# Latent heads of a two-block layer: where the exponent table is loaded, when a gate bank is read, and in which bank finished pairs are turned

## The chip, the cores and the metric

The kernel runs on one core of one Trainium2 chip. The metric is the device time of one execution in microseconds (us). Five engines work side by side: TensorE (PE in the profile, with its weight loads as PEld), VectorE (DVE), ScalarE (ACT), GpSimd (POOL) and SyncE (SP), which issues the transfers of the weights. Each engine takes its instructions strictly in the order in which the program lists them, and an instruction waits there until its semaphores have reached their values.

## What is computed

Two transformer blocks in a row on 512 tokens of width 1024, all in float32 precision. The first block has a gated convolution, a sparse attention, a cross attention and a feed-forward. The second block is the one that the change touches: its mixer has an mLSTM (4 heads) beside a latent attention (8 heads), whose outputs are joined and projected.

```python
def causal_block_attention(q, k, v):
    ...
    sc = jnp.einsum('bhqd,bkhd->bhqk', qblk.astype(jnp.float32), kf) * scale
    sc = jnp.where(kpos[None, :] <= qpos[:, None], sc, -jnp.inf)
    p = jax.nn.softmax(sc, axis=-1)
    return jnp.einsum('bhqk,bkhd->bqhd', p, vf)

def token_mixer(a, ...):
    proj = a @ w_in                       # q, k, v, output gate o_ml and gates of the mLSTM, latents
    ...
    h_ml = mlstm_chunkwise(...)
    h_ml = rmsnorm(h_ml, ...) * jax.nn.sigmoid(o_ml)
    ...
    h_mla = causal_block_attention(q, k, kv[..., MLA_NOPE:])
    return jnp.concatenate([h_ml, h_mla], axis=-1) @ w_out
```

## The kernel before

**Weights.** All matrices are streamed as 256 chunks of 512 KB through a ring of four slots (`w_raw`). SP issues chunk c when the products of chunk c-4 are done (`chunk_done`). ACT rounds a chunk to `w_hi` (`round_to`, L1205, with the cast at L1203), POOL subtracts to get the rest `w_lo` (L405), and PE multiplies in three products (hi by hi, hi by lo, lo by hi, L494). One chunk against all 512 tokens is 8 steps of three products of 512 columns.

**The latent tiles.** The attention of 8 heads runs over 32 tiles: tile n is head n // 4 and query block n % 4, so it has n % 4 + 1 blocks of 128 keys. For a tile, PE makes the scores (`latent_scores`, banks 4 and 5), DVE adds the mask and finds the maximum (`latent_mask`), ACT takes the exponential (`latent_exps`), PE turns it (`latent_turn`, bank 6), ACT copies it (`latent_turned`), PE multiplies it with the values (`latent_values`, bank 2) and DVE scales the result into `o_rows` (`latent_scaled`). In loop n PE makes the scores of tile n+2, turns tile n and makes the values of tile n-1.

**What runs beside them.** Bank 7 (`BESIDE_BANK`) gets 56 steps of three products: four row blocks of the mLSTM's values (steps 0 to 31) and three chunks of its output gate (steps 32 to 55, `gate_step`). The table `BESIDE` says how many of these steps PE does in loop n, and `BESIDE_DONE` in which loop DVE reads the finished bank (`beside_out`; the gates by `gate_out`, L2278). The first gate chunk, OA, is made ahead of the tiles, in another bank, and its reading by DVE stands between the first masks and loop 0. The four mLSTM heads follow each other every seven loops (`ml_step`); of their steps PE makes products with `sT`, ACT makes `decay`, squares and a root (which needs another function table than the exponential), and DVE the rest.

**Pairs.** After 8 tiles two heads are finished. PE turns the pair's rows (`pair_turn`, L1017) into bank 2, ACT casts them to `mix_hi` (`pair_hi`, L1639), and DVE subtracts to get `mix_lo` (`pair_lo`, L2411). Bank 2 is also the bank of the values, so in the loops n = 9, 17 and 25 the values of tile n-1 are put off to the next loop, where they wait until `pair_lo` has read the bank (`o_ready`). The fourth pair comes behind the last tile. Behind the tiles the output projection (`wo_step`) begins, and the last mLSTM head is turned between its steps (`ml_turn`, L967).

## Time and profile before

| | us |
|---|---|
| median of 3 runs | 1586.34 |
| lowest and highest of them | 1584.93, 1586.52 |
| time of the profiled execution | 1584.47 |
| its span, from first to last instruction | 1582.7 |
| mean granted TensorE clock | 0.997 of full speed |

The profile is one execution. The stage that the change touches lies between about 1035 and 1180 us from the start of the span. Starts and durations are of the profile; the end of a matmul is modelled and lies some 0.16 us behind the point at which the next one can start, so the idle time that a row names in brackets is smaller than the time lost between starts.

### The profile page before, as it was taken

Reading aid. Unit: us, or ns where it says so; the run is one execution under the profiler, and the core shown is the slowest. Engines: PE = TensorE matmul, PEld = TensorE weight load, DVE = VectorE, ACT = ScalarE, POOL = GpSimd, SP = SyncE. Lnnn points to the kernel's source line nnn. Section 1 sums busy time; section 2 is a strip of 40 time slices with the busy share of each in tenths; the row PEclk is TensorE's granted clock in tenths of the full one; section 3 lists DMA queues with packets and bytes.
Section 4 is the critical chain, followed back from the end, with each engine's and each line's share of the span. In section 5 each row is a group of like instructions: output and inputs, shape, how many; then the busy total and the mean of one; then the engine's idle time right before and its main releaser. Section 6 shows DMA issues by size and latency. Waiting matters only on the chain.

```text
span 1582.7 us, 21175 instructions
## 1 busy us (share of the span) xinstructions
PE 1546.7 (98%) x7370; PEld 1280.5 (81%) x7370; DVE 838.8 (53%) x1483; ACT 652.6 (41%) x1065; POOL 662.9 (42%) x301
## 2 busy tenths in 40 slices
PE   7999999999999999999999999999999999999997
PEld 6888888778788877888888888777779888888887
DVE  5689999887784445442111134767645612121125
ACT  5553333444462445433233245455754523232331
POOL 4454444323334432444444445442524544444442
PEclk9999999999999999999999999999999999999999
DMA  5243323221333322333333333221112333333332
...
DMA packets 41125, 144.57 MB, mean 91 GB/s; under 512 B 4565, under 2 KB 6741, under 8 KB 40793
## 3 DMA queue, kind: packets, MB, share of 16 engines
...
q14 instruction: 29, 0.23, 0.1%
...
## 4 chain that ended last, share of the span: by engine, by line
PE 90%; issue 3%; DVE 3%; ACT 2%; POOL 1%; DMA 1%; SPq 0%; DVEq 0%; POOLq 0%; ACTq 0%
PE bank L494 88%; DMA w_raw<-in_stream 1%; PE bank L604 1%; POOL w_lo L405 1%; POOL res L470 1%; DVE x_sq L1807 1%; PE bank L999 0%; DVE bias L1880 0%; DVE xu_lo L1816 0%; ACT w_hi L1203 0%; ACT kT L1368 0%; DVE ffy L2574 0%; ACT probs L1236 0%; DVE kh L2377 0%; DVE q_ml L2351 0%
## 5 line engine op out<-in xcount | busy, mean ns | idle before, releaser
L405 POOL TENSOR_TENSOR w_lo<-w_raw,w_hi 128x1024 fp32r<-128x1024 f32 x254 | 614.4, 2419 | 847.3 <-ACT w_hi L1203 847.1
L1203 ACT CAST w_hi<-w_raw 128x1024 fp32r<-128x1024 f32 x256 | 268.6, 1050 | 501.6 <-DMA w_raw<-in_stream 501.5
L494 PE MATMUL bank<-a_hi,w_hi 128*128 128x512 f32 (+1 forms) x1120 | 445.0, 397 | 2.9 <-DVE a_lo L2487 1.7
L494 PE MATMUL bank<-a_hi,w_lo 128*128 128x512 f32 (+1 forms) x1120 | 431.6, 385 | 0.0
L494 PE MATMUL bank<-a_lo,w_hi 128*128 128x512 f32 (+1 forms) x1120 | 431.2, 385 | 0.0
L494 PEld LDWEIGHTS bank<-a_hi,w_hi 128*128 128x128 f32 x1120 | 210.5, 188 | 50.7 <-issue 4.1
L494 PEld LDWEIGHTS bank<-a_lo,w_hi 128*128 128x128 f32 x1120 | 210.5, 188 | 45.7 <-issue 3.6
L494 PEld LDWEIGHTS bank<-a_hi,w_lo 128*128 128x128 f32 x1120 | 210.3, 188 | 42.2
L494 PE MATMUL bank<-b_hi,w_hi 128*128 128x512 f32 (+1 forms) x640 | 244.3, 382 | 0.0
L494 PE MATMUL bank<-b_hi,w_lo 128*128 128x512 f32 (+1 forms) x640 | 242.3, 379 | 0.0
L494 PE MATMUL bank<-b_lo,w_hi 128*128 128x512 f32 (+1 forms) x640 | 242.2, 378 | 0.0
L494 PEld LDWEIGHTS bank<-b_hi,w_hi 128*128 128x128 f32 x640 | 120.4, 188 | 22.7 <-issue 0.2
L494 PEld LDWEIGHTS bank<-b_lo,w_hi 128*128 128x128 f32 x640 | 120.4, 188 | 22.6 <-issue 0.2
L494 PEld LDWEIGHTS bank<-b_hi,w_lo 128*128 128x128 f32 x640 | 120.4, 188 | 22.6
L2113 DVE SCALAR_TENSOR_TENSOR ff_t<-bank,rstd 128x512 f32<-128x512 f32 x64 | 44.2, 690 | 149.1 <-PE bank L494 149.1
L2116 DVE TENSOR_TENSOR b_lo<-ff_f,b_hi 128x512 fp32r<-128x512 f32 x64 | 47.2, 738 | 86.8 <-ACT b_hi L1472 86.8
L1944 DVE SCALAR_TENSOR_TENSOR bank<-conv_in,cols,bank 128x512 f32<-128x512 f32 x114 | 82.3, 750 | 1.6
L2124 DVE TENSOR_TENSOR res<-bank,res 128x512 f32<-128x512 f32 x32 | 22.1, 691 | 108.7 <-PE bank L494 108.7
L1923 DVE SCALAR_TENSOR_TENSOR bank<-conv_in,cols,bank 128x512 f32<-128x512 f32 x116 | 76.6, 749 | 0.0
L1470 ACT ACTIVATE ff_f<-ff_t 128x512 f32<-128x512 f32 x64 | 40.5, 632 | 85.6 <-DVE ff_t L2113 85.6
L2124 DVE TENSOR_TENSOR ffy<-bank,ffy 128x512 f32<-128x512 f32 x20 | 13.8, 692 | 84.4 <-PE bank L494 84.4
L1245 ACT COPY probsT<-bank 128x256 f32<-128x256 f32 (+3 forms) x48 | 19.7, 409 | 58.0 <-PE bank L604 58.0
...
## 6 DMA issues: line engine op xcount, KB each, us to landing
w_raw<-in_stream SPq DMA_DIRECT2D x256, 512.0 KB, 3.5
...
```

Source lines behind the costliest of these rows:

```text
L405: nc.gpsimd.tensor_tensor(w_lo[:, j, :], w_raw[:, j, :], w_hi[:, j, :].bitcast(F32), ALU.subtract).then_inc(w_lo_done, 1)
L470: nc.gpsimd.tensor_tensor(res[:, j, t], res[:, j, t], mixed[:, j, t], ALU.add).then_inc(sems["post_added"], 1)
L494: return nc.tensor.matmul(o, l, r, start=start, stop=stop)
L604: m = nc.tensor.transpose(turned_bank(U)[:, r], probs[:, U % 2, r], ident)
L1203: A.copy(w_hi[:, slot, :], w_raw[:, slot, :]).then_inc(w_hi_done, 1)
L1245: A.copy(probsT[:, U % 2, r], turned_bank(U)[:, r]).then_inc(sems["pT_copied"], 1)
L1470: A.activation(ff_f[:, j % 2, :], ff_t[:, j % 2, :], ACT.Square).then_inc(sems["f_sq"], 1)
L1923: V.scalar_tensor_tensor(out=blk(conv_io, e, 0, T) if last else acc, in0=u, scalar=w, in1=acc, op0=ALU.mult, op1=ALU.add).then_inc(sems["c ...
L1944: m = V.scalar_tensor_tensor(out=out, in0=u, scalar=w, in1=acc if start is None else start, op0=ALU.mult, op1=ALU.add)
L2113: V.scalar_tensor_tensor(out=ff_t[:, j % 2, :], in0=bank, scalar=0.0, in1=rstd[:, :], op0=ALU.max, op1=ALU.mult).then_inc(evac_dve, 1)
L2116: V.tensor_tensor(b_lo[:, j, :], ff_f[:, j % 2, :], b_hi[:, j, :].bitcast(F32), ALU.subtract).then_inc(sems["f_ready"], 1)
L2124: V.tensor_tensor(dst[:, i, :], bank, dst[:, i, :], ALU.add).then_inc(evac_dve, 1)
```

## The change

It has three parts. First, ACT gets a dummy exponential of one column (`table_first`) ahead of `round_to(CH["OA"])`, so that the table is loaded there. Second, DVE reads the OA bank (`gate_out(0, ...)`) ahead of the last of three gate-row operations, not behind it, and the small memset of `v_ml` goes ahead of both. Third, the first three pairs are turned into bank 7 in loops 10, 17 and 25 (`PAIR_TURN_AT`), in which `BESIDE` has no step; the values are no longer put off, and instead the first step of each of the last three gate chunks waits for `pair_lo` (`o_ready`). `pair_hi` now stands behind the copy and the exponential of its loop on ACT, and `pair_lo` behind `latent_scaled` on DVE. `BESIDE`, `BESIDE_DONE` and `cast_at` are laid anew: from loop 11 on steps move to later loops, five of them into loops 28 to 30.

```diff
```diff
--- before.py
+++ after.py
@@ -144,8 +144,9 @@
 ML_END = ML_EVERY * (ML_HEADS - 1) + ML_START + 13
 
 
-BESIDE = [3, 3, 2, 4, 4, 4, 4, 3, 3, 2, 0, 2, 2, 2, 1, 1, 2, 1, 2, 1, 1, 1, 2, 1, 2, 1, 1, 1]
-BESIDE_DONE = {2: 0, 4: 1, 6: 2, 9: 3, 15: 4, 21: 5, 27: 6}
+BESIDE = [3, 3, 2, 4, 4, 4, 4, 3, 3, 2, 0, 1, 2, 2, 1, 1, 1, 0, 1, 1, 2, 1, 1, 1, 1, 0, 1, 2, 2, 2, 1]
+PAIR_TURN_AT = {10: 0, 17: 1, 25: 2}
+BESIDE_DONE = {2: 0, 4: 1, 6: 2, 9: 3, 16: 4, 24: 5, 30: 6}
 BESIDE_BANK = 7
 CONV_AT = {0: 0, 4: 1}
 SILU_AT = {4: (0, 2), 14: (1, 3)}
@@ -351,6 +352,9 @@
                 return ps[2][:, :], c_hi[:, G, :], c_lo[:, G, :]
             return ps[2][:, :], xo_hi[:, G - X_G, :], xo_lo[:, G - X_G, :]
 
+        def pair_bank(p):
+            return ps[BESIDE_BANK if p < MLA_HEADS // 2 - 1 else 2]
+
         def turned_bank(U):
             return ps[6 + U % 2]
 
@@ -923,6 +927,7 @@
                 c, o = CH["OM"] + j, O["OM"] + j
                 if k == 0:
                     pe.wait_ge(evac_dve, o - DVE_FROM)
+                    pe.wait_ge(sems["o_ready"], MLA_G + j + 1)
                 chunk(c, c % RING, None, BESIDE_BANK, a_hi, a_lo, ks=range(k, k + 1))
 
             def beside(n):
@@ -1002,10 +1007,7 @@
             def latent_values(n):
                 h, nk = n // 4, n % 4 + 1
                 pe.wait_ge(sems["pT_copied"], U0 + n + 1)
-                if n % 8 == 0:
-                    pe.wait_ge(sems["o_ready"], MLA_G + n // 8)
-                else:
-                    pe.wait_ge(sems["o_scaled"], n)
+                pe.wait_ge(sems["o_scaled"], n)
                 for kb in range(nk):
                     m = mm(ps[2][:, 0:MLA_V], probsT[:, n % 2, kb * P:(kb + 1) * P],
                            v_mla[kb // 2][:, kb % 2, h * MLA_V:(h + 1) * MLA_V], kb == 0, kb == nk - 1)
@@ -1013,8 +1015,10 @@
 
             def pair_turn(p):
                 pe.wait_ge(sems["o_scaled"], 8 * p + 8)
+                if p < MLA_HEADS // 2 - 1:
+                    pe.wait_ge(evac_dve, O["OM"] + p - DVE_FROM)
                 for qb in range(TB):
-                    m = nc.tensor.transpose(ps[2][:, qb * P:(qb + 1) * P], o_rows[p][:, qb, :], ident)
+                    m = nc.tensor.transpose(pair_bank(p)[:, qb * P:(qb + 1) * P], o_rows[p][:, qb, :], ident)
                 m.then_inc(sems["o_turned"], 1)
 
             c, o = CH["OA"], O["OA"]
@@ -1028,14 +1032,11 @@
             for n in range(4 * MLA_HEADS):
                 if n + 2 < 4 * MLA_HEADS:
                     latent_scores(n + 2)
-                turning = n >= 8 and n % 8 == 1
-                if n >= 8 and n % 8 == 2:
-                    latent_values(n - 2)
+                if n in PAIR_TURN_AT:
+                    pair_turn(PAIR_TURN_AT[n])
                 ml_hook(n)
-                if turning:
-                    pair_turn(n // 8 - 1)
                 latent_turn(n)
-                if n >= 1 and not turning:
+                if n >= 1:
                     latent_values(n - 1)
                 ml_turns(n)
             latent_values(4 * MLA_HEADS - 1)
@@ -1555,6 +1556,7 @@
                 for i in range(4):
                     A.copy(qh[rr, 4 * t + i, :], qrot[ROPE * i:ROPE * (i + 1), t, :]).then_inc(sems["q_roped"], 1)
             round_to(CH["UKV"])
+            A.activation(table_first[:, :], eps, ACT.Exp)
             round_to(CH["OA"])
 
             def ml_step(h, st):
@@ -1590,7 +1592,7 @@
                     act.wait_ge(sems["ml_gated"], h + 1)
                     A.copy(mix_hi[h], hml[:, h % 2, :]).then_inc(sems["ml_hi"], 1)
 
-            cast_at = {8: CH["VM"] + 1, 9: CH["VM"] + 2, 10: CH["VM"] + 3, 11: CH["OM"], 16: CH["OM"] + 1, 22: CH["OM"] + 2, 28: CH["WO"]}
+            cast_at = {8: CH["VM"] + 1, 9: CH["VM"] + 2, 10: CH["VM"] + 3, 11: CH["OM"], 18: CH["OM"] + 1, 26: CH["OM"] + 2, 32: CH["WO"]}
 
             def ml_hook(n):
                 if n == 0:
@@ -1636,18 +1638,18 @@
 
             def pair_hi(p):
                 act.wait_ge(sems["o_turned"], p + 1)
-                A.copy(mix_hi[ML_HEADS + p], ps[2][:, :]).then_inc(sems["o_hi"], 1)
+                A.copy(mix_hi[ML_HEADS + p], pair_bank(p)[:, :]).then_inc(sems["o_hi"], 1)
 
             latent_exps(0)
             latent_exps(1)
             open_gate(0)
             round_to(CH["VM"])
             for n in range(4 * MLA_HEADS):
-                if n >= 8 and n % 8 == 1:
-                    pair_hi(n // 8 - 1)
                 latent_turned(n)
                 if n + 2 < 4 * MLA_HEADS:
                     latent_exps(n + 2)
+                if n in PAIR_TURN_AT:
+                    pair_hi(PAIR_TURN_AT[n])
                 ml_hook(n)
             pair_hi(MLA_HEADS // 2 - 1)
             for n in range(4 * MLA_HEADS, ML_END):
@@ -2408,29 +2410,26 @@
 
             def pair_lo(p):
                 dve.wait_ge(sems["o_hi"], MLA_G + p + 1)
-                V.tensor_tensor(mix_lo[ML_HEADS + p], ps[2][:, :], mix_hi[ML_HEADS + p].bitcast(F32), ALU.subtract
+                V.tensor_tensor(mix_lo[ML_HEADS + p], pair_bank(p)[:, :], mix_hi[ML_HEADS + p].bitcast(F32), ALU.subtract
                                 ).then_inc(sems["o_ready"], 1)
 
             latent_mask(0)
             latent_mask(1)
             chained(V.tensor_tensor(gt[g4, 0, :], gt[g4, 0, :], gt[g4, 3, :], ALU.subtract))
             chained(V.tensor_tensor_scan(gt[g4, 4, :], gt[g4, 5, :], gt[g4, 0, :], 0.0, ALU.add, ALU.max))
-            V.tensor_tensor(gt[g4, 3, :], gt[g4, 3, :], gt[g4, 4, :], ALU.add).then_inc(sems["gates_done"], 1)
+            V.memset(v_ml[:, :, :, ML_V:ML_V + 1], 1.0).then_inc(sems["ml_ones"], 1)
             dve.wait_ge(chunk_done, CH["OA"] + 1)
             gate_out(0, ps_of(O["OA"]))
-            V.memset(v_ml[:, :, :, ML_V:ML_V + 1], 1.0).then_inc(sems["ml_ones"], 1)
+            V.tensor_tensor(gt[g4, 3, :], gt[g4, 3, :], gt[g4, 4, :], ALU.add).then_inc(sems["gates_done"], 1)
             for n in range(4 * MLA_HEADS):
                 latent_inverse(n)
                 if n + 2 < 4 * MLA_HEADS:
                     latent_mask(n + 2)
-                turning = n >= 8 and n % 8 == 1
-                if n >= 8 and n % 8 == 2:
-                    latent_scaled(n - 2)
-                if turning:
-                    pair_lo(n // 8 - 1)
                 ml_first(n)
-                if n >= 1 and not turning:
+                if n >= 1:
                     latent_scaled(n - 1)
+                if n in PAIR_TURN_AT:
+                    pair_lo(PAIR_TURN_AT[n])
                 ml_rest(n)
             latent_scaled(4 * MLA_HEADS - 1)
             pair_lo(MLA_HEADS // 2 - 1)
```
```

The order of the instructions shows the three places of which the prediction speaks. Ahead of tile 0, on ACT, before (`w_hi` is the cast of a weight chunk, the first `probs` rows are the exponentials of tiles 0 and 1, `ogate` the gate of OA):

```order
L1203 CAST w_hi<-w_raw 128x1024 [waits chunk_done,raw_landed3]
L1628 ACT_TABLE_LOAD [waits p_inv,pT_ready]
L1628 ACTIVATE probs,rowsum<-bank,negmax 128x128 [waits s_masked]
L1628 ACTIVATE probs,rowsum<-bank,negmax 128x256 [waits p_inv,pT_ready,s_masked]
L1537 ACTIVATE ogate<-ogate 128x512 [waits evac_dve]
L1539 ACTIVATE ogate<-ogate,half_gain 128x512 [waits o_gated]
L1203 CAST w_hi<-w_raw 128x1024 [waits chunk_done,raw_landed0]
```

The same place after the change; the load stands ahead of the cast whose data the transfer brings last:

```order
L1559 ACT_TABLE_LOAD
L1559 ACTIVATE table_first<-consts 128x1
L1204 CAST w_hi<-w_raw 128x1024 [waits chunk_done,raw_landed3]
L1630 ACTIVATE probs,rowsum<-bank,negmax 128x128 [waits p_inv,pT_ready,s_masked]
L1630 ACTIVATE probs,rowsum<-bank,negmax 128x256 [waits p_inv,pT_ready,s_masked]
L1538 ACTIVATE ogate<-ogate 128x512 [waits evac_dve]
L1540 ACTIVATE ogate<-ogate,half_gain 128x512 [waits o_gated]
L1204 CAST w_hi<-w_raw 128x1024 [waits chunk_done,raw_landed0]
```

What moved is the table load, from directly ahead of the first exponential to ahead of the cast. On DVE, at the same time, before (`gt` are rows of the gates, the row with `ogate<-bank` reads the OA bank):

```order
L2416 TENSOR_TENSOR gt<-gt 4x512
L2417 SCALAR_TENSOR_TENSOR gt<-gt 4x512 [waits row_step]
L2418 TENSOR_TENSOR gt<-gt 4x512 [waits row_step]
L2278 TENSOR_TENSOR ogate<-bank,ssq 128x512 [waits chunk_done]
L2421 MEMSET v_ml 128x16
L2400 RECIPROCAL rowinv<-rowsum 128x1 [waits p_ready]
L2394 ISA bank,negmax<-bank,consts 128x384 [waits p_ready,s_ready]
```

And after; the third row with `gt` now stands behind the reading of the bank:

```order
L2418 TENSOR_TENSOR gt<-gt 4x512
L2419 SCALAR_TENSOR_TENSOR gt<-gt 4x512 [waits row_step]
L2420 MEMSET v_ml 128x16 [waits row_step]
L2280 TENSOR_TENSOR ogate<-bank,ssq 128x512 [waits chunk_done]
L2423 TENSOR_TENSOR gt<-gt 4x512
L2402 RECIPROCAL rowinv<-rowsum 128x1 [waits p_ready]
L2396 ISA bank,negmax<-bank,consts 128x384 [waits p_ready,s_ready]
```

What moved is that one row, behind the bank's reading. On PE, loops 9 to 11, before (`o_rows` is the turning of pair 0, `v_mla` with `probsT` the values, the last row the first gate step in bank 7; the first of the four transposes of the turning is the row ahead of these):

```order
L1017 MATMUL bank<-consts,o_rows_162 128x128 x3
L999 MATMUL bank<-consts,probs 128x128 [waits pT_copied,p_ready]
L999 MATMUL bank<-consts,probs 128x128
L494 MATMUL bank<-kh,qh 128x128 [waits q_roped,rope_done,p_ready]
L494 MATMUL bank<-v_mla_127,probsT 128x64 [waits o_ready,pT_copied]
L494 MATMUL bank<-v_ml,sT 128x129 [waits ml_ones,evac_dve,ml_sT]
L999 MATMUL bank<-consts,probs 128x128 [waits pT_copied,p_ready]
L999 MATMUL bank<-consts,probs 128x128 x2
L494 MATMUL bank<-v_mla_127,probsT 128x64 [waits o_scaled,pT_copied]
L494 MATMUL bank<-v_mla_127,probsT 128x64
L494 MATMUL bank<-kh,qh 128x256 [waits p_ready]
L494 MATMUL bank<-a_hi,w_hi 128x512 [waits w_lo_done,evac_dve]
```

And after, up to the same gate step:

```order
L1004 MATMUL bank<-consts,probs 128x128
L498 MATMUL bank<-v_mla_127,probsT 128x64 [waits o_scaled,pT_copied]
L498 MATMUL bank<-kh,qh 128x128 [waits q_roped,rope_done,p_ready]
L1021 MATMUL bank<-consts,o_rows_162 128x128 [waits evac_dve,o_scaled]
L1021 MATMUL bank<-consts,o_rows_162 128x128 x3
L498 MATMUL bank<-v_ml,sT 128x129 [waits ml_ones,evac_dve,ml_sT]
L1004 MATMUL bank<-consts,probs 128x128 [waits pT_copied,p_ready]
L1004 MATMUL bank<-consts,probs 128x128 x2
L498 MATMUL bank<-v_mla_127,probsT 128x64 [waits o_scaled,pT_copied]
L498 MATMUL bank<-v_mla_127,probsT 128x64
L498 MATMUL bank<-kh,qh 128x256 [waits p_ready]
L498 MATMUL bank<-a_hi,w_hi 128x512 [waits w_lo_done,o_ready,evac_dve]
```

What moved: the turning stands behind tile 9 and the scores of tile 12, the values of tile 8 no longer wait for `o_ready`, and the gate step does. On ACT, loops 16 and 17, before (`mix_hi` is the cast of pair 1):

```order
L1203 CAST w_hi<-w_raw 128x1024 [waits chunk_done,raw_landed1]
L1567 DMA mrow<-m_rows 128x512 [waits ml_decay,ml_diag]
L1537 ACTIVATE ogate<-ogate 128x512 [waits evac_dve]
L1539 ACTIVATE ogate<-ogate,half_gain 128x512 [waits o_gated]
L1639 CAST mix_hi_150<-bank 128x512 [waits o_turned]
L1635 COPY probsT<-bank 128x256 [waits pv_done,pT_ready]
L1628 ACTIVATE probs,rowsum<-bank,negmax 128x512 [waits p_inv,pT_ready,s_masked]
L1583 ACTIVATE ml_square,mcol<-bank 128x128 [waits ml_out]
L1583 ACTIVATE ml_square,mcol<-bank 128x128 x3
L1635 COPY probsT<-bank 128x384 [waits pv_done,pT_ready]
```

And after:

```order
L1569 DMA mrow<-m_rows 128x512 [waits ml_decay,ml_diag]
L1637 COPY probsT<-bank 128x256 [waits pv_done,pT_ready]
L1630 ACTIVATE probs,rowsum<-bank,negmax 128x512 [waits p_inv,pT_ready,s_masked]
L1641 CAST mix_hi_150<-bank 128x512 [waits o_turned]
L1585 ACTIVATE ml_square,mcol<-bank 128x128 [waits ml_out]
L1585 ACTIVATE ml_square,mcol<-bank 128x128 x3
L1538 ACTIVATE ogate<-ogate 128x512 [waits evac_dve]
L1540 ACTIVATE ogate<-ogate,half_gain 128x512 [waits o_gated]
L1637 COPY probsT<-bank 128x384 [waits pv_done,pT_ready]
L1630 ACTIVATE probs,rowsum<-bank,negmax 128x128 [waits p_inv,pT_ready,s_masked]
L1204 CAST w_hi<-w_raw 128x1024 [waits chunk_done,raw_landed1]
```

What moved: the cast of pair 1 stands behind the copy and the exponential of its loop, the gate's two operations behind the mLSTM's squares, and the weight cast to loop 18.

## Rows read from the trace of the kernel before

**Rows 1.** The page's first part: busy us, share of the span, instructions

```profile
PE 1546.7 (98%) x7370; PEld 1280.5 (81%) x7370; DVE 838.8 (53%) x1483; ACT 652.6 (41%) x1065; POOL 662.9 (42%) x301
```

**Rows 2.** PE's waits, 1040 to 1190: us in total, times, longest

```profile
PE bank L494 <- DVE mix_lo L2411: 3.2, 3, 1.1
```

**Rows 3.** Timeline, loops 9 to 12, PE, POOL and DVE

```profile
1094.86 0.39 PE L494 MATMUL bank<-kh,qh 128*128 128x128 f32 x2
1096.30 0.41 PE L494 MATMUL bank<-v_mla,probsT 128*128 128x64 f32 x2 [1.05 <-DVE mix_lo L2411]
...
1097.39 4.89 POOL L405 TENSOR_TENSOR w_lo<-w_raw,w_hi 128x1024 fp32r<-128x1024 f32 x2 [2.56 <-ACT w_hi L1203]
...
1098.70 3.86 DVE L2377 COPY kh<-krT 32x512 f32<-32x512 f32 x2
...
1104.23 1.08 PE L494 MATMUL bank<-v_mla,probsT 128*128 128x64 f32 x8 [0.82 <-DVE o_rows L2406]
```

**Rows 4.** Stretch by engine: us, PE, PEld, DVE, ACT, POOL, clock, DMA, GB/s

```profile
1053.30:1056.70 3.40, 3.19 (x8) 2.54 (x9) 2.16 (x9) 2.38 (x3) 0.81 (x1) 0.50 0.11 45
1094.30:1096.40 2.10, 1.05 (x10) 0.89 (x9) 0.94 (x2) 1.56 (x5) 0.54 (x1) 1.00 0.64 168
```

**Rows 5.** PE's timeline before tile 0: start, us, instruction, [idle before it]

```profile
1050.11 0.39 PE L494 MATMUL bank<-a_hi,w_lo 128*128 128x512 f32 x1
1051.20 0.91 PE L494 MATMUL bank<-kh,qh 128*128 128x384 f32 x2 [0.69 <-ACT probs L1628]
1053.51 0.76 PE L494 MATMUL bank<-w_hi,a_hi 128*128 128x512 f32 x1 [1.40 <-DVE ogate L2278]
...
1056.91 0.40 PE L494 MATMUL bank<-w_hi,a_lo 128*128 128x512 f32 x1
```

**Rows 6.** The same stretch, timeline of ACT, POOL and DVE

```profile
1048.32 1.05 ACT L1203 CAST w_hi<-w_raw 128x1024 fp32r<-128x1024 f32 x1 [2.89 <-DMA w_raw<-in_stream]
...
1049.39 1.28 ACT L1628 ACT_TABLE_LOAD   x1
...
1049.45 2.78 POOL L405 TENSOR_TENSOR w_lo<-w_raw,w_hi 128x1024 fp32r<-128x1024 f32 x1 [1.56 <-ACT w_hi L1203]
...
1050.10 2.67 DVE L2418 TENSOR_TENSOR gt<-gt 4x512 f32<-4x512 f32 x1
...
1052.69 0.67 DVE L2278 TENSOR_TENSOR ogate<-bank,ssq 128x512 f32<-128x512 f32 x1
```

**Rows 7.** The memsets of `q_ml` (min/median/max ns), and POOL at 1107

```profile
L2385 DVE MEMSET q_ml<- x4: 485/485/485, 1070.2 to 1108.4; 64x512 f32 x4
...
1107.09 2.04 POOL L434 TENSOR_TENSOR res<-res,cols 128x512 f32<-128x512 f32 x2
```

**Rows 8.** Timeline, loops 16 to 18: PE, DVE, ACT

```profile
1116.04 0.86 PE L494 MATMUL bank<-kh,qh 128*128 128x384 f32 x2
...
1117.42 2.66 DVE L2351 SCALAR_TENSOR_TENSOR q_ml<-q_ml,qk_ml 64x512 f32<-64x512 f32 x2
1120.11 1.66 DVE L2351 SCALAR_TENSOR_TENSOR qk_ml<-k_tanh,qk_ml 128x512 f32<-128x512 f32 x1
...
1123.47 0.38 ACT L1635 COPY probsT<-bank 128x256 f32<-128x256 f32 x1
1123.61 0.69 DVE L2411 TENSOR_TENSOR mix_lo<-bank,mix_hi 128x512 fp32r<-128x512 f32 x1 [0.72 <-ACT mix_hi L1639]
1123.74 0.70 ACT L1628 ACTIVATE probs<-bank,negmax 128x512 f32<-128x512 f32 x1
...
1124.45 0.41 PE L494 MATMUL bank<-v_mla,probsT 128*128 128x64 f32 x2 [1.05 <-DVE mix_lo L2411]
1124.66 0.47 PE L494 MATMUL bank<-a_hi,w_hi 128*128 128x512 f32 x1
```

**Rows 9.** Timeline behind the last tile: PE, ACT, DVE, PE

```profile
1167.63 0.66 PE L1017 MATMUL bank<-consts,o_rows 128*128 128x128 f32 x4 [0.45 <-DVE o_rows L2406]
...
1170.07 0.17 DVE L2319 SCALAR_TENSOR_TENSOR mcol<-mcol 128x4 f32<-128x4 f32 x1
```

## The prediction

> **What bounds the kernel now.** I read the page's busy times first: PE is busy for 98% of the span [rows 1], so nothing that another engine does counts unless PE waits for it. Then the waits of PE alone, in the stretch that the change touches: PE waited 3.2 us for `mix_lo`, three times, once at each of the first three pairs [rows 2]. The brackets understate what is lost. For pair 0 the row says 1.05 [rows 3], but the scores ahead started at 1094.86 and take 0.22, and the next product started at 1096.30: 1.22 us between starts. Summed in that way, from one start to the next against the usual 0.23 us of a product, I find 13.4 us lost between 1050 and 1168: 4.1 around the first tiles, 6.6 in loops 10 to 26, 2.7 in the last loops. This is all that the change can win. Last the clock: for 3.4 us from 1053.30 on PE was granted half of it, 1.2 of 2.4 GHz; around pair 0 it kept the whole [rows 4].
>
> **Part 1, the table load and the OA bank.** Ahead of the first step in bank 7 stand two waits [rows 5]. The scores of tile 2 wait for the first exponential, which waits for the table load of 1.28 us; and the first step waits for DVE to read OA's bank, which DVE does only at 1052.69, since the gate row ahead of it took 2.67 us beside a subtraction of POOL's [rows 6]. After the change the load falls into ACT's 2.89 us of idle time ahead of the cast at 1048.32, which waits for its transfer and so does not move. The first exponential then starts near 1049.4 and not at 1050.69, and the scores of tile 2 find it done. The Trainium skill (ScalarE: Activation LUTs, "ACT is a hardware spline evaluator", under what a load costs) states 1283 ns for the load and about 1380 ns of drain behind it. The trace has the 1.28 but starts the exponential 0.02 us behind it. By the page's 2.66 us the gain would not be larger than the sum below, because the bank is what comes last; and the load with its drain would still fit into the 2.89.
>
> DVE can read the bank when OA's last product ends, 1050.11 + 0.39 = 1050.50 [rows 5]; the reading is a form with one operand in the accumulator banks, which took 0.67 us at 1052.69. The memset now ahead of it isn't held up by POOL: those of `q_ml` took 485 ns at 1070 with POOL idle and 485 ns at 1108 with POOL busy [rows 7]. From the start of the reading to PE's first step it was 1053.51 - 1052.69 = 0.82 us, so PE starts at 1051.3: 2.2 us earlier. And PE then idles for 0.4 us and not 2.4 in those 3 us, so the clock shouldn't fall: nine products took 3.64 us (eight starts from 1053.51 to 1056.91, and one more), at 0.23 each and 0.1 for the first it is 2.15: 1.5 us. What is late next: the last value chunk's rest is needed in loop 2; its transfer starts with OA's end and takes some 3.5 us, an estimate, cast and subtraction 1.05 + 2.78 more [rows 6], which is 1057.8, when PE gets there. I count 0.1. The gate row that was passed (now ending near 1052.8 again, held by the same subtraction of POOL's) is needed in loop 1 only. **Sum -3.6** (bounds -2.1, if the clock falls all the same, and -4.1, all that was lost).
>
> **Part 2, pairs 0 and 1.** No instruction is added or removed: four turnings, a cast and a subtraction per pair, as before. The wait isn't removed either. It moves from the values to the first gate step one loop later, and the chain in it grows: the turning's cast stands on ACT behind the copy and the exponential of its loop. For pair 0 my walk along the queues gives 2.1 us of waiting where there were 1.22. But a little later both versions wait for the same thing: DVE's two copies of `kh` took 3.86 us beside two subtractions of POOL's, and PE got the next values only at 1104.23 [rows 3]. The weight cast that feeds POOL comes some 0.6 us earlier, so that point comes 0.8 us earlier, but with one step (three products, 0.69 us) less done. Net -0.1.
>
> For pair 1 I count from the scores of tile 18 at 1116.04. Before, PE was at the gate step of loop 18 at 1124.66, 8.6 us later [rows 8]. After: DVE has mask 18, then the three operations of L2351, which took 4.35 us from 1117.42 beside POOL and start at the same point, since both engines wait for the same scores: done at +5.7. Then the gate bank's reading, which the new table puts here (0.69), `sT` and the scaling of tile 15: +6.7. Only then may PE turn the pair; by its own work it is there at +3.9, so it idles for 2.9 us. Turning 0.44, two products with `sT` 0.22, turning of tile 17 0.22: +7.7. ACT: 0.2 to start, copy 0.27 (1123.47 to 1123.74), exponential 0.67 (0.70 less an overlap) [rows 8], cast 0.6: +9.45. DVE and back to PE 0.84, as from the `mix_lo` at 1123.61 to the row at 1124.45: +10.3. That is 1.7 us later, with two steps (1.4 us) less done: +3.1. **Sum of both pairs +3.0** (bounds 0, if other work covers the longer chain, and +4).
>
> **Part 3, pair 2 and the end.** Pair 2 goes like pair 0, without the wait for the copies; two table loads that stood directly ahead of the copy of tile 25 now come beside gate steps. **+0.2.** The last loops: before, PE had no step in loops 28 to 31 and waited five times, the last with 0.45 in brackets [rows 9]; 2.7 us between starts. Five steps now lie in loops 28 to 30 and cover the first three waits: **-1.3** (bounds -2.7 and 0). Behind the last pair ACT gets a weight cast of 1.05 us ahead of the last head's root. The turning of that head stands between steps of the projection and has a little slack, so I take half of the 1.05: **+0.5** (bounds 0 and +2.3, below).
>
> **Part 4, the clock.** PE would idle for 2.9 us ahead of pair 1 and, after 1.2 us of work, for 2.1 more. Around OA, idling for 2.4 of 3 us brought it to half [rows 4, 5]; at pair 0, 1.2 of the 1.44 us up to 1096.30 didn't [rows 3, 4]. I take one fall, at the price that the nine products paid plus a little for the small ones: **+1.7** (bounds 0 and +2.6).
>
> **Sum.** -3.6 + 3.0 + 0.2 - 1.3 + 0.5 + 1.7 = +0.5 us. The profiled execution of 1584.47 us would become 1585.0. The median of before is 1586.34, so 1.9 us above the profiled execution; the same step on it gives **1586.8 us**. A measurement of this kernel can tell about 0.2%, 3.2 us, from no change, so my forecast is no change that can be told.
>
> **Rivals.**
> - *The pair waits are covered.* Part 1 stands, the pairs cost no more than before and the clock stays up: -3.6 + 0 + 0.2 - 1.3 + 0.5 = -4.2, 1582.1 us. For it: part 1 is the surest term, and ACT is busy for 41% of the span [rows 1], so away from the pairs little is queued ahead of a cast. Against it: in loops 16 and 17 the chain over DVE is longer than PE's work by 2.9 us even with nothing added.
> - *The clock falls at all three pairs* (the slower side). The waits of 2.1 and 2.3 us at pairs 0 and 2 lie between the 1.2 that left the clock up and the 2.4 that brought it down. Each further fall costs 1.7: +0.5 + 3.4 = +3.9, 1590.2 us. [...]
> - *A shared port at the end.* The cast moved behind the last pair gives POOL a subtraction that starts near 1169.95; DVE's small product of two operands from the same memory started at 1170.07 [rows 9]. The gate row of only four partitions was held from 1050.10 until POOL was through [rows 6]. If this one is held too, the root comes 1.8 us later still: +2.3, 1588.6 us. The Trainium skill (SBUF — State Buffer, "SBUF: two separate sides") gives this as a rule: VectorE with two SBUF inputs and GpSimd share one pair of ports, and whoever starts first holds it for the whole instruction. By that rule, the trace agrees in [rows 6], and only the 0.1 us between the two starts decides.
> - *The change doesn't do what it says:* the load is hidden, but the clock falls around OA as before. Then part 1 is -2.1: +2.0, 1588.3 us.
>
> **How the numbers follow.** Forecast 0.45 (1584 to 1589.5 of its own); covered 0.25; three falls 0.15; port 0.10; clock around OA 0.05. The range from 1581.5 to 1591 takes in all but the outer halves of the first two rivals. Faster by over 0.2%: 0.25, the covered case. Slower by over 0.2%: 0.15 of the clock, and 0.07 for the port and the forecast's upper end with a second mishap: 0.22. Within: 0.53.
>
> **What would show it.** Part 1: the load near 1045.5, PE's first step in bank 7 near 1051.3, no half clock near 1053. Part 2: PE waits at the first gate steps for `mix_lo`, longer than 1.05 in brackets each; ahead of pair 1's turning PE waits for DVE. Part 3: no waits in loops 28 to 30. Part 4: a half-clock stretch near 1118 to 1123. If PE doesn't wait ahead of pair 1, or the waits at the gate steps are under 1 us, part 2 is wrong and the time falls towards 1582.

## The result

| | us |
|---|---|
| before, median of 9 runs | 1586.12 (1584.39 to 1586.84) |
| after, median of 9 runs | 1590.05 (1588.37 to 1593.53) |
| ratio | 1.0027, 95% interval 1.0018 to 1.0035 |
| profiled execution after, and its span | 1590.11, 1588.3 |

The changed kernel is slower by 0.27%, 3.9 us of the medians. The time lies inside the range given, but it isn't the forecast (1586.8, no change that can be told): it is slower by more than a measurement's uncertainty. It lies 0.5 us above the forecast's own upper end (1589.5); that the range of 9.5 us takes it in says little for the sum. It falls almost on the rival of three clock falls (1590.2), and yet not for that rival's reasons.

The page of the changed kernel has PE 3.4 us busier than [rows 1], with the same 7370 matmuls:

```profile
PE 1550.1 (98%) x7370; PEld 1282.8 (81%) x7370; DVE 842.3 (53%) x1483; ACT 652.7 (41%) x1066; POOL 661.4 (42%) x301
```

PE's waits in the changed kernel from 1040 to 1190 (total, times, longest) answer to [rows 2]. The three waits for `mix_lo` are now named "issue"; they stand at the gate steps, 0.05 to 0.1 us behind `mix_lo`. Two are new, ahead of a turning of a pair (L1021) and of the last head (L972):

```profile
PE bank L498 <- issue: 5.6, 3, 1.9
PE bank L1021 <- DVE o_rows L2408: 3.1, 2, 2.7
PE bank L498 <- DVE o_rows L2408: 1.2, 2, 0.7
PE bank L972 <- DVE ml_rows L2342: 0.6, 1, 0.6
```

**The first place.** Timeline before tile 0, which answers to [rows 5, 6]:

```profile
1047.38 1.28 ACT L1559 ACT_TABLE_LOAD   x1
1048.68 0.20 ACT L1559 ACTIVATE table_first<-consts 128x1 f32<-128x1 f32 x1
...
1052.03 0.39 PE L498 MATMUL bank<-a_hi,w_lo 128*128 128x512 f32 x1
...
1052.30 0.91 PE L498 MATMUL bank<-kh,qh 128*128 128x384 f32 x2
1052.46 0.69 DVE L2280 TENSOR_TENSOR ogate<-bank,ssq 128x512 f32<-128x512 f32 x1 [0.32 <-PE bank L498]
...
1053.07 1.70 DVE L2423 TENSOR_TENSOR gt<-gt 4x512 f32<-4x512 f32 x1
...
1053.30 0.47 PE L498 MATMUL bank<-w_hi,a_hi 128*128 128x512 f32 x1
```

From OA's last product to the first step in bank 7 it is 1.27 us, where it was 3.40. The dummy exponential starts 0.02 us behind the load's end. The Trainium skill (ScalarE: Activation LUTs, "ACT is a hardware spline evaluator") adds a drain of about 1.38 us to a load; it doesn't show here either.

**Pair 1.** Loops 16 to 18 of the changed kernel, PE, DVE and ACT, which answer to [rows 8]:

```profile
1114.99 2.66 DVE L2353 SCALAR_TENSOR_TENSOR q_ml<-q_ml,qk_ml 64x512 f32<-64x512 f32 x2
...
1117.69 1.64 DVE L2353 SCALAR_TENSOR_TENSOR qk_ml<-k_tanh,qk_ml 128x512 f32<-128x512 f32 x1
1119.25 0.68 DVE L2280 TENSOR_TENSOR ogate<-bank,ssq 128x512 f32<-128x512 f32 x1
...
1120.37 0.66 PE L1021 MATMUL bank<-consts,o_rows 128*128 128x128 f32 x4 [2.66 <-DVE o_rows L2408]
...
1121.48 0.44 PE L498 MATMUL bank<-kh,qh 128*128 128x128 f32 x2
...
1123.07 0.69 DVE L2413 TENSOR_TENSOR mix_lo<-bank,mix_hi 128x512 fp32r<-128x512 f32 x1 [1.03 <-ACT mix_hi L1641]
...
1123.86 0.76 PE L498 MATMUL bank<-a_hi,w_hi 128*128 128x512 f32 x1 [1.94 <-issue]
```

PE loses 2.8 us ahead of the turning and 2.1 ahead of the gate step (between starts), and the clock falls at 1122.55, within the second of these waits.

**The last head.** Behind the last tile, ACT, POOL, DVE and PE, which answers to [rows 9]:

```profile
1171.90 1.05 ACT L1204 CAST w_hi<-w_raw 128x1024 fp32r<-128x1024 f32 x1
...
1173.03 2.37 POOL L409 TENSOR_TENSOR w_lo<-w_raw,w_hi 128x1024 fp32r<-128x1024 f32 x1 [10.34 <-ACT w_hi L1204]
1173.16 2.27 DVE L2321 SCALAR_TENSOR_TENSOR mcol<-mcol 128x4 f32<-128x4 f32 x1
...
1177.29 0.66 PE L972 MATMUL bank<-consts,ml_rows 128*128 128x128 f32 x4 [0.62 <-DVE ml_rows L2342]
```

DVE's product on four columns starts 0.13 us behind POOL's subtraction and takes 2.27 us instead of 0.17.

**The clock.** Stretches of the changed kernel (the granted clock is the third column from the end), which answer to [rows 4]: none at the first place, one behind pair 1, one behind the last tile:

```profile
1050.50:1054.00 3.50, 3.42 (x14) 2.19 (x13) 3.06 (x5) 2.75 (x7) 2.16 (x1) 1.00 0.14 9
1122.50:1129.20 6.70, 5.34 (x17) 4.40 (x18) 3.34 (x18) 5.94 (x17) 1.20 (x1) 0.50 0.00 0
1170.40:1173.90 3.50, 3.50 (x11) 2.93 (x12) 1.79 (x6) 2.69 (x4) 0.87 (x1) 0.52 0.00 0
```

### The profile page after: what moved, and what is told of

Same layout as the page of the kernel before. It is cut to its first block, busy times and chain, and to the rows that moved or that the text cites. A ratio compares the mean times of both kernels' runs of the same rounds, so it can differ in the third digit from the quotient of the medians.

```text
span 1588.3 us, 21179 instructions
## 1 busy us (share of the span) xinstructions
PE 1550.1 (98%) x7370; PEld 1282.8 (81%) x7370; DVE 842.3 (53%) x1483; ACT 652.7 (41%) x1066; POOL 661.4 (42%) x301
## 3 DMA queue, kind: packets, MB, share of 16 engines
HBM read 141.43 MB, written 2.11 MB: 90 GB/s over the span
## 4 chain that ended last, share of the span: by engine, by line
PE 89%; DVE 4%; issue 3%; ACT 2%; POOL 1%; DMA 1%; SPq 0%; DVEq 0%; POOLq 0%; ACTq 0%
PE bank L498 87%; PE bank L608 1%; DMA w_raw<-in_stream 1%; POOL w_lo L409 1%; POOL res L474 1%; DVE x_sq L1809 1%; PE bank L1004 1%; DVE cq_rstd L1745 0%; DVE xu_lo L1818 0%; DVE bias L1882 0%; ACT w_hi L1204 0%; ACT kT L1369 0%; DVE cn_lo L2230 0%; DVE gt L2253 0%; DVE ffy L2573 0%
```

## The experiments

All ratios are to the kernel before on the same chip; their intervals reach 1.3 to 2.2 us to either side, so the runs can't tell two kernels apart that differ by about a microsecond. Shifts are read from one trace each: the start of the same matmul against the profile of before, in three pieces: from OA's last product to loop 9 (1050.11 to 1092.38 in the kernel before), from there to the turning of pair 3 (1167.63), and from there to 1180.01.

| kernel | to loop 9 | to pair 3 | end | stage | ratio (95%) |
|---|---|---|---|---|---|
| changed | -3.6 | +4.4 | +2.4 | +3.2 | 1.0027 (1.0018 to 1.0035) |
| e8 changed again | -3.6 | +5.1 | +2.5 | +3.9 | 1.0033 (1.0021 to 1.0046) |
| e1 part 1 | -3.6 | 0.0 | 0.0 | -3.6 | 0.9992 (0.9983 to 1.0001) |
| e2 changed without part 1 | -1.5 | +5.4 | +2.2 | +6.2 | 1.0049 (1.0035 to 1.0063) |
| e3 last cast at 33 | -3.6 | +4.4 | 0.0 | +0.8 | 1.0019 (1.0010 to 1.0028) |
| e4 pair's cast first | -3.6 | +3.1 | +2.0 | +1.5 | 1.0019 (1.0010 to 1.0028) |
| e5 new tables, old pairs | -3.7 | +3.0 | 0.0 | -0.7 | 1.0029 (1.0018 to 1.0041) |
| e6 products in loop 15 | -3.6 | +1.5 | +2.0 | -0.1 | 1.0010 (1.0001 to 1.0019) |
| e7 scan late, on before | -1.5 | +0.1 | 0.0 | -1.4 | 0.9991 (0.9982 to 1.0000) |
| e9 load only | -1.5 | 0.0 | 0.0 | -1.5 | 0.9996 (0.9987 to 1.0006) |
| e10 bank first only | -3.3 | 0.0 | +1.6 | -1.7 | 0.9996 (0.9987 to 1.0005) |
| e11 change mended | -3.7 | -1.8 | 0.0 | -5.5 | 0.9971 (0.9960 to 0.9982) |
| e12 part 1, scan, products | -3.4 | +0.8 | +1.6 | -1.1 | 0.9988 (0.9978 to 0.9997) |

**e1_part1 and e2_pairs_only** split the change in two. e1's edit on the kernel before (e2 takes the same lines out of the changed kernel):

```diff
             round_to(CH["UKV"])
+            A.activation(table_first[:, :], eps, ACT.Exp)
             round_to(CH["OA"])
...
-            V.tensor_tensor(gt[g4, 3, :], gt[g4, 3, :], gt[g4, 4, :], ALU.add).then_inc(sems["gates_done"], 1)
+            V.memset(v_ml[:, :, :, ML_V:ML_V + 1], 1.0).then_inc(sems["ml_ones"], 1)
             dve.wait_ge(chunk_done, CH["OA"] + 1)
             gate_out(0, ps_of(O["OA"]))
-            V.memset(v_ml[:, :, :, ML_V:ML_V + 1], 1.0).then_inc(sems["ml_ones"], 1)
+            V.tensor_tensor(gt[g4, 3, :], gt[g4, 3, :], gt[g4, 4, :], ALU.add).then_inc(sems["gates_done"], 1)
```

> Part 1 alone on the kernel before (table load ahead of the cast of OA, bank of OA read ahead of the third gate row, pairs and tables as before). My theory: this part did what was forecast, and all of the loss comes from the pairs. PE's first step in bank 7 comes 3.6 us earlier against the last product of OA, no half clock near 1053, no half clock near 1122 or 1170 either, and the time is 3.7 us below before: about 1582.4, ratio 0.9977. Rival: the half-clock stretches near 1122 and 1170 of the changed kernel belong to a stage that is run more densely from 1053 on, whatever the pairs do. Then they appear here too, and the time is 1584.5 to 1586, ratio 0.999 to 1.000.

> The changed kernel without part 1 (load directly ahead of the first exponential, OA bank read behind the third gate row), pairs and tables as in the changed kernel. My theory: the losses add up, so it is 3.7 us above the changed kernel: 1593.7, ratio to before 1.0048; half clock near 1053, at pair 1 and perhaps at the end. Rival: the clock falls at pair 1 only because it was not already low near 1053. Then the time is 1591 or less, ratio 1.003.

e1's trace shows the 3.6 us and no half clock in the stage, so both falls of the changed kernel come with the rest. But its runs give 1.3 us and not 3.7, and their interval takes in no change at all. e2 shows one reason: it has before's two waits at the first place, 0.73 and 1.69 us between starts, and its clock did not fall there (-1.5 in the table); e7, with the same order, had no fall there either. So in one of three traces with these waits the clock fell, the one of before, and 1.5 of my 3.6 us were that fall. A second reason lies in e1's own executions: the profiled one is the fastest of eleven (1582.50, mean clock 0.998), and the mean clock of all eleven is 0.9966, below the 0.9968 of before's on that chip. So the other ten, at 0.995 to 0.997, lost some clock that the trace doesn't show; where, no trace says. e10 and e12 below, its nearest relatives, lost 1.6 us of it near 1168. How much of the gap each reason makes stays open. e2's ratio came as expected, by another sum.

**e3_cast33** moves one cast:

```diff
-            cast_at = {8: CH["VM"] + 1, 9: CH["VM"] + 2, 10: CH["VM"] + 3, 11: CH["OM"], 18: CH["OM"] + 1, 26: CH["OM"] + 2, 32: CH["WO"]}
+            cast_at = {8: CH["VM"] + 1, 9: CH["VM"] + 2, 10: CH["VM"] + 3, 11: CH["OM"], 18: CH["OM"] + 1, 26: CH["OM"] + 2, 33: CH["WO"]}
```

> The changed kernel with the last weight cast of the stage one loop later (33 for 32), so behind the root of the last mLSTM head on ACT, and POOL's subtraction with it. My theory (shared port and the cast in front of the root cost 0.8 us at the last head): DVE's product on 4 columns takes 0.17 us again and not 2.27, PE no longer waits for the turning of the last head, the time is 0.8 us below the changed kernel: 1589.2, ratio to before 1.0020. The half clock near 1170 starts before the cast and stays. Rival: the cast's place costs nothing, since the slow clock alone makes PE late or early there; the time is that of the changed kernel, 1590.0, ratio 1.0025, and PE's wait ahead of the turning stays over 0.5 us.

Timeline of e3 at the place of the changed kernel's last rows:

```profile
1173.88 0.16 DVE L2321 SCALAR_TENSOR_TENSOR mcol<-mcol 128x4 f32<-128x4 f32 x1
...
1174.39 1.03 ACT L1204 CAST w_hi<-w_raw 128x1024 fp32r<-128x1024 f32 x1
...
1175.50 2.40 POOL L409 TENSOR_TENSOR w_lo<-w_raw,w_hi 128x1024 fp32r<-128x1024 f32 x1 [11.61 <-ACT w_hi L1204]
...
1176.09 0.60 PE L972 MATMUL bank<-consts,ml_rows 128*128 128x128 f32 x4
```

The product takes 0.16 us and PE waits for nothing. The gain in the trace is 2.4 us, larger than the 0.8 expected. The runs give 1.3 to 2.2 us (the changed kernel has 1.0027, and 1.0033 as e8 on another chip), with intervals that overlap e3's. e4 and e6 say why: there the clock stayed up behind the last tile, PE came to the turning sooner, and waited 2.0 us, as in these rows of e4:

```profile
1172.48 2.40 POOL L409 TENSOR_TENSOR w_lo<-w_raw,w_hi 128x1024 fp32r<-128x1024 f32 x1 [9.90 <-ACT w_hi L1204]
...
1172.61 2.30 DVE L2321 SCALAR_TENSOR_TENSOR mcol<-mcol 128x4 f32<-128x4 f32 x1
...
1176.77 0.66 PE L972 MATMUL bank<-consts,ml_rows 128*128 128x128 f32 x4 [1.81 <-DVE ml_rows L2342]
```

So the cast's place costs 2.0 us with a full clock; where the clock falls, slow products cover a part of it and the sum is 2.4.

**e4_hi_first** puts the pair's cast ahead on ACT:

```diff
+                if n in PAIR_TURN_AT:
+                    pair_hi(PAIR_TURN_AT[n])
                 latent_turned(n)
                 if n + 2 < 4 * MLA_HEADS:
                     latent_exps(n + 2)
-                if n in PAIR_TURN_AT:
-                    pair_hi(PAIR_TURN_AT[n])
```

> The changed kernel with the cast of the turned pair ahead of the copy and the exponential of its loop on ACT (as in the kernel before), everything else as changed. My theory (the wait at the first gate step is the chain turning, copy, exponential, cast, subtraction, and the operations queued ahead of the cast are its price): the wait ahead of the gate step falls from 2.1 us between starts to some 1.2 at each of the three pairs, the wait of 2.8 us ahead of pair 1's turning stays since it is DVE's; if the clock then still falls at pair 1, the time is 2.7 us below the changed kernel, 1587.3, ratio 1.0008; if it stays up, 2.5 less, 1584.8, ratio 0.9993. Rival: the copy that is now late makes the products with the values late, and the wait only moves: 1589.5 or more, ratio 1.002.

From the start ahead of a gate step to its own it was 2.13, 2.22 and 2.22 us at the three pairs in the changed kernel; here it is 1.40, 1.09 and 1.61. The wait ahead of pair 1's turning stayed at 2.8. But behind pair 0 the wait for `o_rows` grew from 0.84 to 1.58, which is the rival in part. The gain to pair 3 is 1.3 us.

**e5_tables_old_pairs** is e1 with the changed kernel's tables, the last cast at 33, and pairs as before (`cast_at` as in e3):

```diff
-BESIDE = [3, 3, 2, 4, 4, 4, 4, 3, 3, 2, 0, 2, 2, 2, 1, 1, 2, 1, 2, 1, 1, 1, 2, 1, 2, 1, 1, 1]
-BESIDE_DONE = {2: 0, 4: 1, 6: 2, 9: 3, 15: 4, 21: 5, 27: 6}
+BESIDE = [3, 3, 2, 4, 4, 4, 4, 3, 3, 2, 0, 1, 2, 2, 1, 1, 1, 0, 1, 1, 2, 1, 1, 1, 1, 0, 1, 2, 2, 2, 1]
+BESIDE_DONE = {2: 0, 4: 1, 6: 2, 9: 3, 16: 4, 24: 5, 30: 6}
```

> The kernel before with part 1 and the new tables of steps (five steps in loops 28 to 30), the last weight cast at loop 33, but the pairs turned in the bank of the values as before. My theory: the tables are worth 1.3 us at the end and the turning in bank 7 is all that costs (5.6 us and the clock at the end). So the time is 1.3 us below part 1 alone, ratio to before 0.9984; no half clock near 1122 or 1170; PE waits 1.2 us at each pair as before. Rival: the tables themselves (fewer steps in loops 11 to 25) are what lets PE idle and the clock fall; then it is 1.0005 or more, and a half-clock stretch lies between 1110 and 1130.

My theory fell here. Without any turning in bank 7, PE stands still in the same place (PE and DVE of e5):

```profile
1116.71 1.08 PE L494 MATMUL bank<-kh,qh 128*128 128x512 f32 x2
1117.77 1.64 DVE L2352 SCALAR_TENSOR_TENSOR qk_ml<-k_tanh,qk_ml 128x512 f32<-128x512 f32 x1
1119.33 0.68 DVE L2279 TENSOR_TENSOR ogate<-bank,ssq 128x512 f32<-128x512 f32 x1
...
1120.26 0.49 PE L494 MATMUL bank<-v_ml,sT 128*128 128x129 f32 x2 [2.48 <-DVE sT L2306]
...
1122.68 0.66 PE L494 MATMUL bank<-v_mla,probsT 128*128 128x64 f32 x2 [1.05 <-DVE mix_lo L2412]
```

and the clock falls behind it, in 1122.60:1126.00, as the granted 0.50 shows:

```profile
1122.60:1126.00 3.40, 3.32 (x13) 2.95 (x13) 1.32 (x10) 3.13 (x14) 0.00 (x0) 0.50 0.00 0
```

Two things in the tables do this, and no run parts them: loops 16 and 17 have two steps less to cover DVE's chain, and the reading of the gate bank (the 0.68 us in the rows) moves from loop 15 into that chain. e3 differs from e5 only in where the pairs are turned: its ratio of 1.0019 against 1.0029, with overlapping intervals, shows no cost of the turning in bank 7, while the traces of the stage have +0.8 against -0.7. The profiled execution of e5 is the fastest of its seven (1584.95; the median is 1590.0, and their mean clocks go from 0.997 down to 0.991, the slowest at 1592.27). Where the others lose the clock no trace shows.

**e6_twice15** takes the three products of DVE out of loop 16:

```diff
-TWICE_AT = {5: 0, 16: 1}
+TWICE_AT = {5: 0, 15: 1}
```

> The changed kernel with the three products of DVE that finish the silu of the second pair of query blocks (L2353, 4.3 us beside POOL) one loop earlier, in loop 15 and not 16; everything else as changed. My theory: these three operations ahead of the gate bank's reading, the sT and the scaling are the wait of 2.8 us ahead of pair 1's turning, and this wait with the 2.1 us behind it brings the clock down. So the wait ahead of the turning is under 0.8 us, part of it comes back as a wait of up to 1 us one loop earlier, no half clock lies near 1124, and the time is 3.5 to 4.5 us below the changed kernel, ratio to before 0.9999 to 1.0005. Rival A: the wait only moves one loop ahead with its full size, the clock falls there: ratio 1.0025. Rival B: the wait goes but the clock falls all the same, from the 2.1 us at the gate step alone: ratio 1.0015.

In loop 15 they take 2.5 us and not 4.3: POOL is idle from 1112.75 to 1114.25, where in the changed kernel two of its operations (2.48 us from 1114.62 on, then 1.71) run beside them:

```profile
1112.20 1.81 DVE L2353 SCALAR_TENSOR_TENSOR q_ml<-q_ml,qk_ml 64x512 f32<-64x512 f32 x2 [1.11 <-ACT q_ml L1618]
...
1114.04 0.69 DVE L2353 SCALAR_TENSOR_TENSOR qk_ml<-k_tanh,qk_ml 128x512 f32<-128x512 f32 x1
...
1115.12 0.49 PE L498 MATMUL bank<-q_ml,qk_ml 128*128 128x128 f32 x2 [0.31 <-DVE sT L2307]
...
1117.81 0.66 PE L1021 MATMUL bank<-consts,o_rows 128*128 128x128 f32 x4
...
1121.30 0.47 PE L498 MATMUL bank<-a_hi,w_hi 128*128 128x512 f32 x1 [1.95 <-issue]
```

The wait of 2.8 us is gone for one of 0.5. The ratio of 1.0010 lies midway between my theory's upper end (1.0005) and rival B (1.0015); the trace decides for B: the clock still falls, at 1121.79, with the wait of 2.1 us ahead of it alone.

**e7_scan_late.** Every trace with the order of before near 1030, ahead of the stage, loses 1.0 to 1.3 us there, the changed kernel's and e1's, e9's and e10's too; only that of before loses nothing. Its timeline, DVE and POOL:

```profile
1027.07 1.21 DVE L2251 TENSOR_TENSOR_SCAN gt<-gt 4x512 f32<-4x512 f32 x1
1027.12 3.37 POOL L405 TENSOR_TENSOR w_lo<-w_raw,w_hi 128x1024 fp32r<-128x1024 f32 x1 [3.28 <-ACT w_hi L1203]
```

and that of the changed kernel, where the scan comes 0.25 us too late:

```profile
1027.58 2.47 POOL L409 TENSOR_TENSOR w_lo<-w_raw,w_hi 128x1024 fp32r<-128x1024 f32 x1 [2.99 <-ACT w_hi L1204]
1027.83 3.30 DVE L2253 TENSOR_TENSOR_SCAN gt<-gt 4x512 f32<-4x512 f32 x1
```

e7 moves the scan in the kernel before:

```diff
-            chained(V.tensor_tensor_scan(gt[g4, 3, :], gt[g4, 1, :], gt[g4, 5, :], 0.0, ALU.add, ALU.add))
             qk_out(2)
             qk_out(3)
+            chained(V.tensor_tensor_scan(gt[g4, 3, :], gt[g4, 1, :], gt[g4, 5, :], 0.0, ALU.add, ALU.add))
```

> The kernel before with one edit ahead of the stage: DVE's scan of a gate row (on 4 partitions) stands behind the reading of the last two query-key banks and not ahead of them. In the profile of the changed kernel the scan took 3.30 us beside POOL and PE lost 1.2 us at 1030; in that of the kernel before it took 1.21 and PE lost nothing. My theory: this is a race of DVE and POOL for who starts first, which a transfer's landing decides by 0.1 us, and has nothing to do with the change. So PE loses nothing near 1030 here, the time is that of the fast half of the runs of before: 0.6 to 1.0 us below its median, ratio 0.9995. Rival: the loss moves to the banks behind it (the scan beside the long memset of POOL), ratio 1.0000 or more.

PE loses nothing near 1030 in e7 and e12, the two kernels with this edit. The changed kernel's 1.3 us there are none of the change's: e10, whose code is that of before up to 1050, loses 1.1.

e7's trace shows one thing more. Its pairs are those of before, PE waits 1.2 us at pair 0 as there, and yet a half clock follows:

```profile
1099.40:1102.70 3.30, 3.30 (x11) 2.54 (x11) 3.27 (x3) 2.17 (x11) 3.29 (x2) 0.50 0.03 11
```

It costs nothing (+0.1 to pair 3 in the table): the slow products fill the 0.98 us that PE otherwise waits for DVE's `o_rows` behind them. The falls at pair 0 in e3 and e6 were free in the same way: e3 has the changed kernel's +4.4.

**e8_changed_again** is the changed kernel.

> The changed kernel once more, on the chip of the experiments, for a second trace. My theory: the waits come back to within 0.1 us (2.1, 2.8 and 2.1, 2.1 between starts), the half clock at pair 1 comes back, the one at 1170 and the loss near 1030 each may be absent; ratio 1.0027. Rival: the half clock at pair 1 is chance as well; then it is absent here.

Waits of 2.83, 1.85 and 2.11 us come back at their places; the half clock at pair 1 begins at 1119.03, some 3 us earlier against the turning, and lasts 10.2 us, not 6.8; the one behind the last tile and the loss near 1030 came back as well.

**e9_load_only and e10_bank_first** each take one half of e1's edit.

> The kernel before with the table load alone moved ahead of the cast of OA; DVE still reads OA's bank behind the third gate row. My theory: PE needs both for its first step in bank 7, and the bank comes last. So the 0.9 us ahead of the scores of tile 2 go, the wait for the bank grows by most of it, the half clock near 1053 stays, and PE's step in bank 7 comes at most 0.3 us earlier against OA's last product. Ratio 0.9997 to 1.0001. Rival: the two waits add up, the load alone gives 0.9 us, ratio 0.9994.

> The kernel before with OA's bank read ahead of the third gate row and the memset ahead of it; the table load stays directly ahead of the first exponential. My theory: the wait for the load (0.9 us ahead of the scores of tile 2) stays, the one for the bank goes or is under 0.3 us; PE idles for 1 us in one piece and the clock stays up, so this edit alone gives 2.5 to 3 us of the 3.65, ratio 0.9980 to 0.9990. Rival: both are needed for the clock; it falls here too, gain 1.3 us, ratio 0.9993.

With the load alone PE still waits for the bank, now in one piece:

```profile
1053.47 2.67 DVE L2419 TENSOR_TENSOR gt<-gt 4x512 f32<-4x512 f32 x1
...
1056.07 0.67 DVE L2279 TENSOR_TENSOR ogate<-bank,ssq 128x512 f32<-128x512 f32 x1
...
1056.88 0.47 PE L494 MATMUL bank<-w_hi,a_hi 128*128 128x512 f32 x1 [2.37 <-DVE ogate L2279]
```

and the clock stayed up: its -1.5 is the same absent fall as in e2 and e7, so the load alone gives nothing. The bank first gives 3.3 - 1.5 = 1.8 us at its place without the load. This is read from one trace each; the runs (0.9996 for both) can tell neither from no change. In e10's trace a half clock came at 1168 that before had not had, and it gave back 1.6:

```profile
1167.30:1171.00 3.70, 3.69 (x12) 3.00 (x13) 1.96 (x10) 2.08 (x3) 0.00 (x0) 0.59 0.00 0
```

**e11_mended** is the changed kernel with the edits of e3, e4 and e6; **e12_best** is e1 with those of e6 and e7.

> The changed kernel with three edits together: DVE's three products one loop earlier (15), the last weight cast at loop 33, the cast of the turned pair ahead of the copy and the exponential of its loop. My theory: the three costs named are all that the change loses, and they add up: 3.5 to 4 us for the products (e6: 1.0010 against 1.0030), 1.9 for the cast (e3), 1 to 2 for the order on ACT (e4). So waits under 0.8 ahead of pair 1's turning and of 1.2 at the gate steps, none ahead of the last head's turning, no half clock from 1050 to 1180, and the time is that of part 1 alone less the tables' 1.3 us at most: ratio 0.9985 to 0.9995. Rival: below the waits named lies another that takes their place; ratio 1.0005 or more.

> Part 1 on the kernel before, with the scan of the gate row behind the last two query-key banks (as in e7) and DVE's three products in loop 15 (as in e6); pairs and tables as before. My theory: part 1 gives 3.6 us in the stage, the scan 0.6 to 1.3, the products 0.5: 1.2 to 5 us below before, by the runs of e1 and e7 (0.9992 and 0.9991) a ratio of 0.9975 to 0.9985. Rival: the runs of part 1 alone gave only 1.3 us, since a half clock that no longer comes near 1053 comes at pair 0 in some executions; then it is 0.9990, with a half-clock stretch near 1095 to 1102 in the trace.

e11 is the fastest of all: 1581.59 us against 1586.3 for the kernel before on its chip, 4.6 us less by the ratio, with no half clock in the stage. That is more than expected (0.9985 to 0.9995; the interval ends at 0.9982), and why isn't shown:

```profile
1050.00:1180.00 130.00, 123.85 (x698) 99.68 (x697) 81.79 (x261) 76.23 (x202) 46.85 (x30) 1.00 0.16 49
```

Its waits of PE from 1040 to 1190 have 3.2 us for `mix_lo` ("issue") and not 5.6, and none ahead of L972:

```profile
PE bank L498 <- issue: 3.2, 3, 1.3
PE bank L498 <- DVE o_rows L2408: 2.0, 2, 1.4
PE bank L1021 <- DVE o_rows L2408: 0.5, 1, 0.5
```

e12 gained less than expected (0.9988 against 0.9975 to 0.9985): in before's table a gate step of loop 15 stands behind the bank that DVE reads behind the three products, and PE waited 1.29 us for it at 1116.84; and a half clock came at 1168. So e6's edit is good with the new tables and bad with the old.

**Do the traces explain the times?** Put 1.5 us onto each stage (the fall that before's profile had there and the other traces don't), and take 1.3 off e7 and e12 for the scan, as if an ordinary execution of before lost the 1.3 us near 1030 too. That gives +4.7 for the changed kernel, +5.4 for e8, -2.1, +7.7, +2.3, +3.0 and +1.4 for e1, e2, e3, e4 and e6, -1.2 for e7, 0.0 and -0.2 for e9 and e10, -4.0 for e11, -0.9 for e12. The ratios say +4.3, +5.2, -1.3, +7.8, +3.0, +3.0, +1.6, -1.4, -0.6, -0.6, -4.6 and -1.9: all within 1.0 us. The two corrections were chosen with the results known, and without the 1.5 the traces lie 0.5 to 2.3 us below the ratios for every kernel but e5, so this shows that the accounts agree, not that each term is right. e5 alone doesn't fit (+0.8 against +4.6); its profiled execution was 5 us below the median of its seven.

## The prediction, point by point

- **What bounds the kernel, and what can be won.** Right: all differences are waits of PE and its clock.
- **Part 1, -3.6.** The trace has 3.64, the waits and the 0.82 us step as forecast. But the step "nine products took 3.64 us, it is 2.15: 1.5 us" took one execution's fall for the rule. The fall is absent from the traces of e2, e7 and e9, which keep that idle time. Without it the trace has 2.1 us; the runs have 1.3, with an interval from a gain of 2.7 to a loss of 0.2. Its two halves aren't equal in the traces: the bank's order gives nearly all of it, the load nothing alone.
- **Part 2, pair 0, -0.1.** Right: 2.1 us at the gate step, 0.84 and not 0.98 for the later values; the lost times of both kernels agree to 0.1 by loop 15.
- **Part 2, pair 1, +3.1.** Right in size: 2.83 + 2.11 us lost against 0.67 + 1.22. My heading blamed the turning for it; e5 shows that the tables alone make a wait of 2.64, at another instruction. The count of "two steps less" had that in it, but the text didn't say that it was the cause.
- **Part 3, pair 2 +0.2, the last loops -1.3.** Right: +0.1 and -1.3.
- **Part 3, the end, +0.5.** Undersized. It cost 2.0 us with a full clock (e4, e6) and is gone in e3. The rival with 0.10, the shared port, came true: in all five traces with the cast at loop 32 POOL starts 0.12 to 0.13 us ahead of DVE's product. The step that failed is "only the 0.1 us between the two starts decides": I took it for a toss and gave it 0.10, but both starts hang on the same cast of the last pair on ACT, and their order came out the same five times. The rule of the Trainium skill (SBUF — State Buffer, "SBUF: two separate sides") is that whoever starts first holds the ports for its whole instruction. The traces agree with it: 2.27 us behind POOL's start (changed kernel), 0.16 without it (e3).
- **Part 4, one clock fall, +1.7.** It began at 1122.55, at the end of the stretch where I had put it, lasted 6.8 us and not 3.4, and cost 2.5 us (e8: 3.2), near the top of its bounds or above it. A second came behind the last tile in the changed kernel, e8 and e2, where I had none, and none in e3, e4, e6 and e11.
- **The sum.** -3.6 + 3.0 + 0.1 - 1.3 + 2.4 + 2.5 = +3.1, against the stage's +3.2; forecast +0.5. The miss of 2.7 is 1.9 at the end and 0.8 of clock. The two profiles differ by 5.6 us: 1.9 more lie ahead of the stage, 1.3 of them at the scan, and 0.6 behind it. The sum had no term for either.
- **The rival of three falls** gave the right number by falls at pairs 0 and 2, which the changed kernel's traces don't have. That the number fits is luck, and where a fall did come at pair 0 (e3, e6, e7), it cost nothing and not 1.7.

## What to carry to other kernels

Before work is moved out of a loop, ask which other engine's chain it covered there: the tables cost here most of what the new bank was blamed for. A small instruction with two operands in the shared memory needs a place where the other user of the port is idle for sure, not one where it wins by 0.1 us. And a clock fall in one profile is worth its price only if a second trace has it too.

## What the chip showed

- The same idle time does and doesn't bring the clock down. 2.52 us between starts in one piece left it at full (e9), as 0.73 and 1.69 did (e2), and 0.85 and 1.56 brought it to half (before). 2.1 us at pair 0's gate step left it up in the changed kernel, e8 and e2, and half clock followed in e3 and e6, and in e7 behind the 1.2 us of before's order. With the 2.6 to 2.8 us of loop 17 it fell in all six traces that have it, in e8 0.65 us before that wait ended.
- A fall can come at a place that no edit touched: e10 and e12 lost 1.6 us near 1168, where neither before nor e1 did. Eight of the 14 traces have a half clock of 3.4 us near 31 us from the start of the span, where all kernels are the same; those of before, the changed kernel and e1 don't. What decides it stays open.
- DVE's scan of four partitions started 0.25 us behind a subtraction of POOL's and took 3.30 us, 0.05 us ahead of it 1.21, and then POOL's took 3.37 for 2.4 to 2.5. In e9 0.05 us behind was enough for 3.41.
